# Feed-forward passes issued in turn for two PSUM banks

## The reference

```python
x = x + mixer(rmsnorm(x))                 # projections, recurrences, output projection
h = rmsnorm(x)                            # (tokens, 1024)
x = x + (silu(h @ w1) * (h @ w3)) @ w2    # w1, w3: 1024 x 2816, w2: 2816 x 1024
y = rmsnorm(x)
```

## Time and profile before

| | |
|---|---|
| median of three runs | 1425.71 us (1424.26 to 1425.88) |
| profiled execution | 1424.7 us |
| its span, first to last instruction | 1422.5 us |
| mean granted TensorE clock | 0.987 of full speed |
| PE busy | 1387.7 us, 98% of the span |
| PEld busy | 1314.3 us, 92% |
| DVE busy | 632.3 us, 44% |
| ACT busy | 361.4 us, 25% |

### The profile page before, as it was taken

How to read it: one execution, slowest core, us unless ns; L and a number is a source line. 1 busy time by engine, 2 the same in 40 slices (tenths; PEclk the granted TensorE clock), 3 DMA queues, 4 the chain that set the end, 5 groups by cost and what they waited for, 6 DMA issues and landing times.

```text
span 1422.5 us, 22617 instructions
## 1 busy us (share of the span) xinstructions
PE 1387.7 (98%) x9774; PEld 1314.3 (92%) x9774; DVE 632.3 (44%) x963; ACT 361.4 (25%) x520; POOL 120.7 (8%) x123
## 2 busy tenths in 40 slices
PE   7999998999999998999999999999999999999997
PEld 6999996899999986999898989898989898989896
DVE  5322359465322379653525252525252525242427
ACT  5212546322222456641011111111111111111114
POOL 0000258100000256000000000000000000000000
PEclk9999999699999999999999999999999999999999
DMA  5621201234221300221010101010101010101003
GB/s 180 178 88 63 89 31 61 90 119 149 89 88 63 119 31 32 84 91 60 30 60 30 59 29 59 29 59 29 59 29 59 29 59 29 59 29 59 29 1 126
DMA packets 28117, 94.59 MB, mean 66 GB/s; under 512 B 2176, under 2 KB 15648, under 8 KB 19232
## 3 DMA queue, kind: packets, MB, share of 16 engines
q1 hardware_dynamic: 28064, 93.81, 18.8%
HBM read 85.81 MB, written 8.00 MB: 66 GB/s over the span
## 4 chain that ended last, share of the span: by engine, by line
PE 93%; DVE 4%; issue 1%; ACT 1%; POOL 1%; DMA 0%; DVEq 0%; SPq 0%; ACTq 0%; POOLq 0%
PE ps L1517 27%; PE ps L1519 27%; PE ps L1518 27%; PE ps L1705 1%; PE ps L1847 1%; PE ps L1820 1%; PE ps L1524 1%; PE ps L1525 1%; PE ps L1760 1%; PE ps L1555 1%; PE ps L1784 1%; PE ps L1789 1%; DVE p_main L1152 1%; DVE b_main L1291 1%; PE ps L1598 0%
## 5 line engine op out<-in xcount | busy, mean ns | idle before, releaser
L1517 PE MATMUL ps<-f_hi,whi 128*128 128x384 f32 (+1 forms) x1056 | 347.9, 329 | 0.6 <-DVE f_lo L1053 0.6
L1518 PE MATMUL ps<-f_lo,whi 128*128 128x384 f32 (+1 forms) x1056 | 347.7, 329 | 0.0
L1519 PE MATMUL ps<-f_hi,wlo 128*128 128x384 f32 (+1 forms) x1056 | 347.6, 329 | 0.0
L1442 DVE TENSOR_TENSOR gated<-gated,ps 128x384 f32<-128x384 f32 (+1 forms) x66 | 35.1, 533 | 402.7 <-ACT gated L939 402.7
L939 ACT ACTIVATE gated<-ps 128x384 f32<-128x384 f32 (+1 forms) x66 | 31.3, 474 | 667.9 <-PE ps L1519 667.8
L1517 PEld LDWEIGHTS ps<-f_hi,whi 128*128 128x128 f32 x1056 | 198.4, 188 | 1.1 <-issue 0.7
L1518 PEld LDWEIGHTS ps<-f_lo,whi 128*128 128x128 f32 x1056 | 198.4, 188 | 0.5
L1519 PEld LDWEIGHTS ps<-f_hi,wlo 128*128 128x128 f32 x1056 | 198.4, 188 | 0.0
L1517 PE MATMUL ps<-h_hi,whi 128*128 128x256 f32 (+1 forms) x624 | 180.2, 289 | 0.5 <-DVE h_lo L1053 0.5
L1519 PE MATMUL ps<-h_hi,wlo 128*128 128x256 f32 (+1 forms) x624 | 179.7, 288 | 0.0
L1518 PE MATMUL ps<-h_lo,whi 128*128 128x256 f32 (+1 forms) x624 | 179.7, 288 | 0.0
(11 more groups left out here) (270 smaller groups left out, 2048.3 us busy)
## 6 DMA issues: line engine op xcount, KB each, us to landing
raw<-in_wstream_f SPq DMA_DIRECT2D x33, 1024.0 KB, 4.8
raw<-in_wstream_a SPq DMA_DIRECT2D x19, 1024.0 KB, 4.8
raw<-in_wstream_b SPq DMA_DIRECT2D x16, 1024.0 KB, 4.8
x_res<-in_x_prompt SPq DMA_DIRECT2D x12, 512.0 KB, 5.0
out_y_prompt<-x_res SPq DMA_DIRECT2D x7, 512.0 KB, 2.6
x_res<-in_state_hgrn SPq DMA_DIRECT2D x4, 512.0 KB, 8.6
val<-in_x_prompt SPq DMA_DIRECT2D x4, 512.0 KB, 5.1
out_new_hgrn_s<-x_res SPq DMA_DIRECT2D x4, 512.0 KB, 5.1
```

The costliest lines, as they stand in the source:

```text
L1442: nc.vector.tensor_tensor(gated[:, s, 0:w], gated[:, s, 0:w], ps[:, 2 * s + 1, 0:w], ALU.mult).then_inc(gm_done, 1)
L1517: nc.tensor.matmul(out, a_hi, b_hi, start=first, stop=False)
L1518: nc.tensor.matmul(out, a_hi, b_lo, start=False, stop=False)
L1519: return nc.tensor.matmul(out, a_lo, b_hi, start=False, stop=last)
```

## The change

`hidden` calls a new function `both_steps(st)` in place of `w1_step(st)` and `w3_step(st)`. It issues the same 48 passes, but for each contraction tile the three kinds in turn for both: w1 into its bank, w3 into the bank behind, and so on. The last w3 pass raises `step_pe`, as before. The two old functions stay for steps 0 and 1 of group 0.

`outputs` treats the two column halves of a token tile together: it waits once, for the addition that frees the second half's bank (two additions further than the old wait of the first half), then issues each kind of pass for both halves, in turn. The last pass of each half raises `y_pe`; these two are now neighbours.

```diff
--- before.py
+++ after.py
@@ -1923,12 +1923,27 @@
                 if end == KT_D:
                     last.then_inc(step_pe, 1)
 
+            def both_steps(st):
+
+                ch, ft = divmod(st, 2)
+                col, w = FF_CHUNKS[ch]
+                a, b = slice(ft * P, (ft + 1) * P), slice(col, col + w)
+                o1, o3 = ps[:, 2 * (st % 2), 0:w], ps[:, 2 * (st % 2) + 1, 0:w]
+                for k in range(KT_D):
+                    first, end = k == 0, k == KT_D - 1
+                    nc.tensor.matmul(o1, w1_hi[:, k, a], f_hi[:, k, b], start=first, stop=False)
+                    nc.tensor.matmul(o3, w3_hi[:, k, a], f_hi[:, k, b], start=first, stop=False)
+                    nc.tensor.matmul(o1, w1_hi[:, k, a], f_lo[:, k, b], start=False, stop=False)
+                    nc.tensor.matmul(o3, w3_hi[:, k, a], f_lo[:, k, b], start=False, stop=False)
+                    nc.tensor.matmul(o1, w1_lo[:, k, a], f_hi[:, k, b], start=False, stop=end)
+                    last = nc.tensor.matmul(o3, w3_lo[:, k, a], f_hi[:, k, b], start=False, stop=end)
+                last.then_inc(step_pe, 1)
+
             def hidden(i, steps):
                 for st in steps:
 
                     pe.wait_ge(gl_done, i * 6 + (st + 1))
-                    w1_step(st)
-                    w3_step(st)
+                    both_steps(st)
 
             def outputs(i):
                 pe.wait_ge(lo_done, i * 3 + (F0_UNIT + 3))
@@ -1936,20 +1951,28 @@
 
                     if n % 3 == 0:
                         pe.wait_ge(gl_done, i * 6 + (2 * (n // 3) + 4))
-                    for q in range(2):
-                        m = 2 * n + q
-                        pe.wait_ge(y_dve, i * 18 + (m + 1))
-                        o = ps[:, 4 + m % 4, :]
-                        for k in range(2):
-                            b = slice(512 * q, 512 * (q + 1))
-                            if t < 8:
-                                a = slice(t * P, (t + 1) * P)
-                                last = three(o, g_hi[:, k, a], g_lo[:, k, a], w2_hi[:, k, b], w2_lo[:, k, b],
-                                             k == 0, k == 1)
-                            else:
-                                last = both(o, g_samp[:, k].rearrange("p e t -> p (e t)"), w2_hi[:, k, b], w2_lo[:, k, b],
-                                            k == 0, k == 1)
-                        last.then_inc(y_pe, 1)
+
+                    m = 2 * n
+                    pe.wait_ge(y_dve, i * 18 + (m + 2))
+                    o = [ps[:, 4 + (m + q) % 4, :] for q in range(2)]
+                    b = [slice(512 * q, 512 * (q + 1)) for q in range(2)]
+                    for k in range(2):
+                        if t < 8:
+                            a = slice(t * P, (t + 1) * P)
+                            for q in range(2):
+                                nc.tensor.matmul(o[q], g_hi[:, k, a], w2_hi[:, k, b[q]], start=(k == 0), stop=False)
+                            for q in range(2):
+                                nc.tensor.matmul(o[q], g_hi[:, k, a], w2_lo[:, k, b[q]], start=False, stop=False)
+                            last = [nc.tensor.matmul(o[q], g_lo[:, k, a], w2_hi[:, k, b[q]], start=False, stop=(k == 1))
+                                    for q in range(2)]
+                        else:
+                            g = g_samp[:, k].rearrange("p e t -> p (e t)")
+                            for q in range(2):
+                                nc.tensor.matmul(o[q], g, w2_hi[:, k, b[q]], start=(k == 0), stop=False)
+                            last = [nc.tensor.matmul(o[q], g, w2_lo[:, k, b[q]], start=False, stop=(k == 1))
+                                    for q in range(2)]
+                    last[0].then_inc(y_pe, 1)
+                    last[1].then_inc(y_pe, 1)
 
 
             pe.wait_ge(lo_done, F0_UNIT + 1)
```

## The result

The changed kernel takes 1428.28 us (median of 20 runs), the kernel before, run beside it, 1424.75: a ratio of 1.0027, 95% interval 1.0020 to 1.0034, so 2.8 to 4.8 us slower. The forecast had +2.4 and the right place, and two thirds of the size.

What follows compares the result with a forecast made beforehand. TensorE, busy 98% of the span with 93% of the chain, was taken to bound the kernel. Turns 0, stalls 10 x 0.20 and tail 0.4 gave +2.4 us on the 1425.71 median: 1428.1, range 1421.0 to 1431.5.

Steps and rivals of the forecast that it cites:

- Turns in the first product: First product: changing bank at every pass, 3072 passes, costs and saves nothing, since existing bank changes keep the beat.
- Turns in the second product: Second product: changing bank at every pass, 1144 passes, costs and saves nothing; steps stay about 0.227 us.
- The merged wait: Second product, last tile of groups 0 to 9: waiting for both late additions costs 0.20 us a group, 2.0 in all.
- The first step: Second product: the last tile starts at 982.07 instead of 981.89, 0.18 us late, behind VectorE's addition.
- The restart: Last tile after the stall: second pass comes 0.25 us later against 0.227, another 0.02; bounds nothing or 0.10.
- The tail: End of the last group: VectorE's last addition comes later, +0.4 us, bounds 0 and 0.5.
- The sum: Whole kernel: 0 + 10 x 0.20 + 0.4 = +2.4 us, median 1428.1 us.
- the case with the most chance, no change: Whole kernel: measured time within about 0.2% (2.9 us) of the kernel before, given 53%.
- Rival 1: First product, groups 1 to 10: the stall brings the fast 384-column beat, -6.4 us, total 1421.7; 13%.
- Rivals 2 and 3: Both products: leaving a bank saves up to 63 us, 1365 (6%); or each turn costs slightly, 4.4 us, 1432.5 (8%).
- rival 4: Last tile: VectorE starts its first addition sooner, no group stalls, only the later end remains, 1426.1; 10%.
- rival 5: Last tile of ten groups: the clock falls to half speed at the new stalls, 27 us, 1455; 1%.

Runs made afterwards that it cites:

- e1: Kernel before with only the first product issued in turns between w1 and w3, pass by pass: 1424.92 against 1424.77 us, ratio 0.9997.
- e5: Changed kernel with the low part of the next w3 made after the sample tile's additions (n == 6): 1424.96 against 1424.63 us, ratio 1.0003.
- e6: Kernel before with the changed kernel's merged wait alone, passes still half after half: 1425.30 against 1424.63 us, ratio 1.0005.
- e4: Changed kernel with each tile's wait split, each half waiting for its own bank, turned order kept: 1426.63 against 1424.77 us, ratio 1.0012.
- e8: Kernel before with one unused 256-column pass ahead of the first product of groups 1 to 10: 1419.48 against 1424.63 us, ratio 0.9962.

## Why the prediction was right, and where it was off

**Turns in the first product, cost 0:** right, by `e1`. The argument from single changes of bank in the old order held for a change at every step.

**Turns in the second product, cost 0:** right. The beat between the passes of the changed kernel is 0.2267 up to the stall, and `e5` has every turn and no loss but the tail.

**The merged wait:** right in place, number and cause. The stall needs the late additions (`e6`), the second low part in its place (`e5`) and, for two thirds of it, the merged wait (`e4`). The first step, 0.18 late, was worked out to the hundredth. (The new wait asks for one addition more than the old wait of the first half, `m + 2` for `m + 1`; the section on the change says two. The working above goes by the right count.)

**The restart: mis-sized.** This is the step that failed: "After such a restart the second pass comes 0.25 later, with 320 columns as with 384: against 0.227 another 0.02." At 512 columns it comes 0.34 later, another 0.11, and the steps after it lose some 0.05 more in the mean of the ten groups (0.02 in group 4): with the 0.18 it is 0.34 us a group and not 0.20. The 0.11 alone is above the 0.10 that I had as the bound of this term, though the whole is inside the 0.35 for a group. I had taken two shapes with one number for a fixed price. The 320 columns of the earlier trace rows take 0.133 us by the clock and the step 0.25, the 512 take 0.213 and the step 0.34: in both the step is the columns' time and 0.12 to 0.13. The 384 columns of the earlier trace rows gave 0.25 from a pass that began 0.03 behind its own weight load; in the other two cases load and pass began together. The load, in the timeline of PEld of the kernel before:

```profile
623.12 0.19 PEld L1517 LDWEIGHTS ps<-f_hi,whi 128*128 128x128 f32 x1 [0.75 <-issue]
```

From there to the second pass at 623.40 it is 0.28, again the columns' 0.160 and 0.12. Counted alike, the two rows would not have agreed at 0.25.

**The tail:** +0.37 for +0.4.

**The sum:** 10 x 0.34 + 0.4 = 3.8 for 2.4. The missing 1.4 us are this one term, and they moved the median over the 0.2% line, on which the interval begins: the case with the most chance, no change, was not what came. Rival 1 fell in its condition (a stall 12 passes ahead does not reach the beat); that the beat can be changed is true, by another way (`e8`). Rivals 2 and 3 fell with `e1` and `e5`; rival 4 would have needed VectorE 0.18 us sooner. Of rival 5: the granted clock of the changed kernel's second product, stall and turns included, is 1.00 (columns as in the earlier trace rows).

```profile
963.70:987.40 23.70, 23.68 (x105) 19.28 (x104) 15.88 (x23) 4.05 (x3) 0.00 (x0) 1.00 0.13 44
```

## What to carry to other kernels

When two results that used to finish one after the other finish together, look at the engine that consumes them: its work starts later by a whole half, and any long instruction queued between decides whether a buffer is free in time; add up that queue against the time of the tiles that really stand in between. Where such a wait misses by a little, price the restart at the width of the pass that restarts, not at another shape's. And before passes are put in another order to save a surplus per pass, see whether that surplus moves at the places where the old order already does what is proposed.

## What the runs showed of the hardware

The 384-column passes have two steady beats, 0.1733 and 0.1767 us, and the kernel stays in the one that it enters with: after the second product's 512 columns in the slow one, with one pass of 256 or 128 columns between in the fast one. A restart in the 512-column passes, 12 passes ahead, does not change it. What holds the slow beat is not settled; stationary operand, moving operand and bank are not it, since its two alternating steps (179 and 174 ns) go on through all of them. In 24 passes of 384 columns no run came nearer to the columns' own time than 13 ns a pass. The formula that the Trainium skill gives for a lone matmul (TensorE: Matmul & The Clock Gate, section Back-to-back issue gap) makes it 162.5 ns at 384 columns, an estimate; neither the turns (176.7 ns) nor the fast beat (173.3 ns) reached it.

TensorE's restart behind VectorE's last addition took 0.06 us in the changed kernel, and a wait that ended 0.10 us before its pass was due still cost 0.07 us one step later (`e4`). The Trainium skill says (TensorE: Matmul & The Clock Gate, section Step-by-step: what each phase is for) that the engine pulls weight loads ahead of running matmuls, where their row groups do not conflict or the load goes to the background weight buffer. The trace of `e4` fits that: the load behind the wait began at 982.58, 0.05 after the addition's end, and not with the pass ahead at 982.40. That the late load makes the 0.07 is argued and not shown: no run here took the load away from the wait.
